# Moving weight buffers and attention operands to other residues modulo 256 bytes in a two-layer fp32 transformer kernel

## What is computed

```python
h = h + 0.5 * swiglu(rms_norm(h, ffn1_norm[i]), ffn1_wgu[i], ffn1_wd[i])   # width 2816
proj = rms_norm(h, mix_norm[i]) @ w_in[i]          # q, k, v, gu, gv, 512 wide each
# differential attention with 4 heads (q, k, v), and chunked spatial gating (gu, gv)
h = h + jnp.concatenate([attn, gm], axis=-1) @ w_out[i]
h = h + cross_attention(rms_norm(h, cross_norm[i]), rms_norm(mem, mem_norm[i]), wq, wkv, wo)
h = h + 0.5 * swiglu(rms_norm(h, ffn2_norm[i]), ffn2_wgu[i], ffn2_wd[i])
```

## Time and profile before

| | before |
|---|---|
| median of three runs | 2208.6 us |
| the profiled execution's own time | 2209.27 us |
| its span, first to last instruction | 2207.3 us |
| mean granted TensorE clock | 0.991 of 2.4 GHz |
| TensorE (PE) busy | 2150.2 us, 97% |
| weight loads (PEld) busy | 1865.0 us, 84% |
| VectorE (DVE) busy | 1504.2 us, 68% |
| ScalarE (ACT) busy | 906.3 us, 41% |
| GpSimd (POOL) busy | 138.8 us, 6% |
| DMA, mean of the span | 96 GB/s |

### The profile page before, as it was taken

The page is one execution under the profiler, slowest core; times in us unless marked ns, Lnnn a source line. Parts: engine busy times, 40 slices in busy tenths (PEclk is TensorE's granted clock), DMA queues, the critical chain, the costliest instruction groups (busy, mean ns, idle before and its releaser), DMA issues. The chain is left out here.

```text
span 2207.3 us, 30029 instructions
## 1 busy us (share of the span) xinstructions
PE 2150.2 (97%) x12251; PEld 1865.0 (84%) x12251; DVE 1504.2 (68%) x2194; ACT 906.3 (41%) x1305; POOL 138.8 (6%) x114
## 2 busy tenths in 40 slices
PE   6999999999999999999989999999999999999998
PEld 5888888788888789888878888978888887888887
DVE  7776775657654777767677776756586456867765
ACT  6343433435434533434343433334454344334332
POOL 0000001100020200000010000021001111000001
PEclk8999999999999999999999999999999999999999
DMA  4333332422221233333223333333132212333331
GB/s 139 98 106 105 93 106 86 134 85 89 96 96 58 67 105 105 101 105 100 86 86 112 90 106 105 96 129 101 58 115 96 77 59 90 98 104 98 105 101 53
DMA packets 267940, 211.96 MB, mean 96 GB/s; under 512 B 7358, under 2 KB 234268, under 8 KB 267804
## 3 DMA queue, kind: packets, MB, share of 16 engines
q1 hardware_dynamic: 264544, 205.55, 29.8%
q10 hardware_dynamic: 3260, 4.51, 0.8%
HBM read 207.93 MB, written 2.10 MB: 95 GB/s over the span
## 5 line engine op out<-in xcount | busy, mean ns | idle before, releaser
L1796 PE MATMUL ps<-hid_hi,wn_hi 128*128 128x512 f32 x592 | 232.6, 393 | 2.4 <-DVE wn_lo L1351 1.7
L1797 PE MATMUL ps<-hid_lo,wn_hi 128*128 128x512 f32 x592 | 231.4, 391 | 0.0
L1798 PE MATMUL ps<-hid_hi,wn_lo 128*128 128x512 f32 x592 | 230.3, 389 | 0.0
L1362 DVE SCALAR_TENSOR_TENSOR h<-ps,h 128x512 f32<-128x512 f32 x224 | 148.4, 686 | 86.4 <-PE ps L1798 83.5
L1797 PE MATMUL ps<-hn_lo,wn_hi 128*128 128x512 f32 x448 | 175.2, 391 | 0.0
L1796 PE MATMUL ps<-hn_hi,wn_hi 128*128 128x512 f32 x448 | 175.2, 391 | 0.0
L1798 PE MATMUL ps<-hn_hi,wn_lo 128*128 128x512 f32 x448 | 174.2, 389 | 0.0
L638 ACT ACTIVATE w_hi<-raw 128x2048 fp32r<-128x2048 f32 x61 | 116.7, 1913 | 124.9 <-PE ps L1798 102.5
L1796 PE MATMUL ps<-hn_hi,w_hi 128*128 128x512 f32 x384 | 154.7, 403 | 9.1 <-DVE Gn L1258 7.1
L1797 PE MATMUL ps<-hn_lo,w_hi 128*128 128x512 f32 x384 | 155.1, 404 | 0.0
L1798 PE MATMUL ps<-hn_hi,w_lo 128*128 128x512 f32 x384 | 155.0, 404 | 0.0
(11 more groups left out here) (323 smaller groups left out, 5910.0 us busy)
## 6 DMA issues: line engine op xcount, KB each, us to landing
raw<-in_ffn_wgu_dram SPq DMA_DIRECT2D x174, 512.0 KB, 4.7
raw<-in_ffn_wd_dram SPq DMA_DIRECT2D x48, 512.0 KB, 3.8
raw<-in_ffn_wd_dram SPq DMA_DIRECT2D x80, 256.0 KB, 3.6
raw<-in_w_in_dram SPq DMA_DIRECT2D x40, 512.0 KB, 4.5
raw<-in_cross_wkv_dram SPq DMA_DIRECT2D x32, 512.0 KB, 3.8
raw<-in_w_out_dram SPq DMA_DIRECT2D x16, 512.0 KB, 3.9
raw<-in_cross_wq_dram SPq DMA_DIRECT2D x16, 512.0 KB, 3.8
raw<-in_cross_wo_dram SPq DMA_DIRECT2D x16, 512.0 KB, 4.2
```

What stands on the lines that cost most here:

```text
L1362: dve.scalar_tensor_tensor(out=h[:, m, :], in0=ps[:, down_bank(c, m), :], scalar=0.5, in1=h[:, m, :], op0=ALU.mult, op1=ALU.add).then_inc( ...
L1796: pe.matmul(dst, a_hi, b_hi, start=start, stop=False)
L1797: pe.matmul(dst, a_hi, b_lo, start=False, stop=False)
L1798: return pe.matmul(dst, a_lo, b_hi, start=False, stop=stop)
```

## The change

Only addresses change. The two paddings behind w_hi and w_lo grow from 128 to 256 bytes, so w_lo goes to residue 0 and the shared area moves up by 256 bytes. form_lo keeps its residue of 192 by a larger offset in w_lo; more_lo goes from 64 to 192; `far` goes from 128 to 256, so its operands go to residue 0. form_hi, more_hi, mg and kc stay at 64. No instruction, order, wait or transfer is added or taken away.

```diff
         w_hi = sb("w_hi", [P, 2, 2048], f32r)
-        top[0] += 128
+        top[0] += 256
         w_lo_at = top[0]
         w_lo = sb("w_lo", [P, 2, 2048], f32r)
-        top[0] += 128
+        top[0] += 256
...
         form_hi = sb("form_hi", [P, 2, 2048], f32r, w_hi_at + 64)
-        form_lo = sb("form_lo", [P, 2, 2048], f32r, w_lo_at + 64)
+        form_lo = sb("form_lo", [P, 2, 2048], f32r, w_lo_at + 192)
...
         more_hi = sb("more_hi", [P, 2, 1536], f32r, sh + 64 * K1 + 64)
-        more_lo = sb("more_lo", [P, 2, 1536], f32r, sh + 76 * K1 + 64)
-        assert sh + 88 * K1 + 64 <= 229344, sh + 88 * K1
+        more_lo = sb("more_lo", [P, 2, 1536], f32r, sh + 76 * K1 + 192)
+        assert sh + 88 * K1 + 192 <= 229344, sh + 88 * K1
...
         odd = sh + 64
-        far = sh + 128
+        far = sh + 256
```

## The result

The changed kernel takes 2189.35 us (median of four runs, 2188.54 to 2189.60) against 2208.53 us before: a ratio of 0.9913, 95% interval 0.9896 to 0.9930. The profiled execution took 2189.42 us, 19.85 less than the one of before. The forecast was 2189 in a range of 2183.5 to 2198.

What follows compares the result with a forecast made beforehand. TensorE was taken as the bound, busy for 2150.2 of 2207.3 us. Gains of 21.9 us, less waits and new settlings, left 19.5 us, from 2209.3 to 2189.8 profiled, 2189 us as median, range 2183.5 to 2198.

Steps and rivals of the forecast that it cites:

- Term 1: hn and hid moving over stationary w, w_lo from 128 to 0: 14 ns a triple, gains of 5.4 and 1.6 us.
- Term 2: Token units, w moving at 0 over hn at 0: 256 triples gain 16 ns each, 4.1 us.
- Term 3: o, qT and gm moving, from 128 to 0, with w at 0: 19 ns a triple, gain 4.9 us.
- Term 4: more_lo from 64 to 192 in the feed-forwards: net 0.123 us per form tile, 48 tiles, gain 5.9 us.
- Term 5: mg with w, and kc by qc, 256 columns: taken as 0, bounds 4 us either way on 960 matmuls.
- Terms 6 and 7: form, t, wn, hid among themselves, and the operands of VectorE, ScalarE and DMA: no change, counted as 0.
- The waits: Gains given back at the wait for rtok, 1.3 us, and for VectorE's additions to h ending each feed-forward, 0.9 us.
- Half of it: Rival: more stays at 117.5 ns, token units only reach 0.687 us a triple; 2197.5 us; chance 0.17 with other partial outcomes.
- Nothing: Rival: wn's lower pace comes from its place, not its address; all terms 0, 2208.6 us; chance 0.04.
- Slower, by a longer period: Rival: true period above 256, say 1024; late units and form with t lose; +13.3 us, 2221.9 us; chance 0.03.

Runs made afterwards that it cites:

- e1_plain: From the kernel before, only w_lo moved to residue 0, form, more and far keeping their residues; 2200.24 us, ratio 0.9964.
- e3_far: From the kernel before, only far moved to residue 0, w_lo staying at 128; 2206.25 us, ratio 0.9992.
- a1_form64: From the changed kernel, form_lo back from 192 to 64, more keeping 64 and 192; 2190.96 us, 0.9921 of the kernel before.
- e0_shift: From the kernel before, shared area moved up by another 256 bytes, all residues modulo 256 kept; 2208.43 us, ratio 1.000.
- b2: From the changed kernel, w_hi to 64 and w_lo to 192, wn staying at 0; 2199.05 us, 0.9960 of the kernel before.

## Why the prediction was right

- *What bounds it.* TensorE was the bound all along. The ledger's sum for the full change is 21.3 us, with the small pairs that the table leaves out; the idle time before TensorE's matmuls, summed over the trace, grew from 49.1 to 50.5, and 19.85 arrived in the profiled execution.
- *Term 1 (hn and hid on w), 7.0 us.* Measured 5.5. The step that was mis-sized is one settled pace for all triples. Of the 1152 matmuls of hn on w, those up to 245 ns apart have a mean of 231.3 before and 227.3 ns after, 4.0 ns of gain and not 4.7. The other 56 gain nothing: they stand at waits, or run at half the clock, where I counted a gain as well. 33 start 400 to 460 ns apart. Twelve of these lie between 48.80 and 53.70 us, where the granted clock was 0.50, the level of 1.2 GHz, after an idle time of 7.1 us; the others follow waits of 2.0 to 6.0 us.
- *Term 2 (token units), 4.1.* Measured 3.9. That w may move at equal residues with hn stationary had no row; it runs at 227.3.
- *Term 3 (o, qT, gm), 4.9.* Measured 4.7, and as an interaction of two parts (e1_plain, e3_far), which the arithmetic of levels had right.
- *Term 4 (more), 5.9.* Measured 3.8 + 1.6 on more and 1.0 on t,form, where the settling of step 6 went: 6.4. The sum was right, with the settling taken too dear (0.03 us where six matmuls at 116.8 instead of 113.3 ns are 0.02), and the stated reason half right. I took 64 and 64 as the cause of the slow pace; a1_form64 shows that it is only a state that did not leave the slow pace once it was entered so.
- *Term 5 (mg, kc), 0 within 4.* Measured a gain of 0.8 and a loss of 0.3. The gain is w moving at equal residues (118.3 to 116.3 ns in e1_plain, 115.8 after). The loss isn't one of kc's and qc's addresses: e1_plain has it without moving them, and e3_far, which moves qc to 0, has a gain. The mean of 281 ns that I took for the slow level is that of one row; the other rows of these pairs have 279 and 280, so they were mixed.
- *Terms 6 and 7.* late units and the pairs on form without a settling moved by nothing, nor did VectorE's work.
- *The waits, 2.2 given back.* The wait for rtok took 0.7 instead of 1.3 us. The wait for VectorE's additions before hid on w went from 4.9 to 5.7 us of idle time, 0.8 where I had 0.9. The errors, 0.9 too much in the gains and about as much in what is given back, cancel: 2189 against 2189.35 is closer than the terms deserve, and that much of it is luck.
- *The rivals.* Half of it: the token units fall to one level and more settles, so no. Nothing: refuted by e0_shift, where the place moves and the time does not, and by b2, where the place stays but for 64 bytes and the time moves. The two independent ports of the page "SBUF — State Buffer" of the Trainium skill, section "Who interferes with whom", would have all of these kernels run alike; they span 2188.7 to 2211.1 us with the same instructions. Slower, by a longer period: refuted by e0_shift, and by the late units of the changed kernel, at the same distance and the same 0.680 us.

## What to carry to other kernels

When TensorE is the bound, read its pace from start to start and compare it between buffers before looking for idle time: 2 to 7 ns a matmul that no wait and no busy share shows were 0.9% here. Place the moving operand and both stationary parts of a rounded float32 product by their differences modulo 256 bytes and by the number of moving columns: equal for 512, stationary parts at 64 and 192 off the moving one for 256. The padding cost nothing here (e0_shift), but a rule found at one length must be measured anew at another.

## What the runs showed of the hardware

- For 512 moving columns of float32 with a fresh weight load each, three matmuls take 0.680 us with all residues equal, and 0.687 to 0.700 us with any of the others tried (one part at 128, all at 128 off, 64 and 192).
- For 256 columns there are three levels: 113.3 ns with stationary parts at 64 and 192, 117.5 or 113.3 with 64 and 64, depending on what ran before, and 120 with both at 0. Other differences, and steps finer than 64 bytes, were not tried on form and more.
- The pace has a memory. After a block of the other length a run needs some six matmuls to reach its own pace (116.8 ns, then 113.3), and with 64 and 64 it stayed slow to its end, 24 matmuls at most, when it was entered so. Why differences of addresses and past timing act together, whether by banks that the two reads share or otherwise, no run here shows.
